# Gathered experts in units of 32 tokens: one row table for both matrices, masks from a unit matrix, quadrants added at a unit's end

## The chip, the cores and the metric

The program runs on one core of a Trainium2 chip. The metric is the device time of one whole execution in microseconds (us), the median of several runs. The engines are TensorE (PE in the profile, PEld its weight loads), VectorE (DVE), ScalarE (ACT), GpSimd (POOL) and SyncE (SP, here only a queue that issues DMAs). PSUM is TensorE's output memory; a DMA moves data between device memory and the on-chip SBUF.

## The reference

The program computes one layer of an encoder for 1,024 prompt tokens and 64 sample tokens, all in float32. The last part of the layer, a mixer over 16,384 tiny experts, takes most of the time and is what the change concerns. Each token chooses 128 experts (8 heads, 16 each); an expert is one row of `peer_u` and one row of `peer_v`, 1,024 wide.

```python
eid = jnp.take_along_axis(cid.reshape(PEER_BLOCK, PEER_HEADS, -1), ci, axis=-1)
gate = jax.nn.softmax(cv, axis=-1).reshape(PEER_BLOCK, -1)
...
u = jnp.take(peer_u, eid, axis=0)
vv = jnp.take(peer_v, eid, axis=0)
a = jax.nn.gelu(jnp.einsum('td,ted->te', xb, u).astype(jnp.float32), approximate=False) * gate
return jnp.einsum('te,ted->td', a.astype(xb.dtype), vv)
```

## The kernel before

The early stages (projection, mixers, routing, a matrix of gates in device memory) end at about 1,770 us of the trace. Then `experts` does the expert mixer in two ways side by side.

**Dense tokens.** For 512 prompt tokens all 16,384 experts are computed, in 64 steps of 256 experts. A float32 product is made of three matmuls of a high part and a low part of each factor. In a step TensorE does 48 matmuls of the U phase (`psum_u`), then 48 of the V phase for the experts of the step before, in 8 groups of 6, each into one bank of `psum_v`. There are 3 such banks: the fourth group of a V phase can only start when VectorE has added the first group's bank into `y`. Around that, in each step: ScalarE applies gelu to each half of the U phase (`act_f`) and writes its high part (`a_hi`), VectorE multiplies by the gates and writes the low part (`a_lo`); when the U phase is over, ScalarE makes the high part of the next U weights (`u_hi`), VectorE the low part (`u_lo`), and after `u_lo` VectorE comes to the eight additions to `y`.

**Gathered tokens.** For the other 512 prompt tokens and the 64 sample tokens only the chosen rows are fetched. GpSimd issues indirect DMAs, each of 128 rows of 4 KB (512 KB): 576 of `u` rows into 6 buffers, 576 of `v` rows into 10. A unit is 64 tokens. On a `u` fetch VectorE does one dot product of 128 rows with the tokens' vectors in `h2n` (one instruction over 128x1024). For `u`, the 128 partitions hold 64 tokens twice (two slots of each), so a unit takes 64 fetches; for `v`, a fetch holds the 128 slots of one token. Between the two the activations must be turned over: once in a unit, ScalarE applies gelu, VectorE multiplies by the gates, TensorE transposes (`turned_g`) and ScalarE copies (`weight`). Then, for every 4 tokens, ScalarE writes 4 masks of 32 columns (one column scaled by the token's weights, the others zero) and TensorE does a **quad**: 8 matmuls with those masks against 4 fetched `v` buffers, which sum up rows in `psum_g`. A tile of 128 tokens is added to `xg` by VectorE and stored (5 tiles in all). The first 80 fetches of `u` come before the first of `v`.

**The order.** Every engine runs its own queue in program order. A class `Timetable` weaves the gathered work into the dense steps: it gives each step 10 places on VectorE, 4 on ScalarE and 4 on TensorE, and puts an item in the first place after its due time (masks in the last place before). 18 fetches (9 of `u`, 9 of `v`) fall due in a step. VectorE's place 3 lies between the gate product of a step's second half and its `a_lo`, place 4 between that `a_lo` and `u_lo`, place 5 between `u_lo` and the first addition to `y`. ScalarE's place 2 lies between the second `a_hi` and `u_hi`. TensorE's place 1 lies between the U and the V phase.

Of the kernel before, what the change touches and what calls it, by code (L numbers as in the profile page):

```python
# [7 lines left out]
F32 = mybir.dt.float32  # L8
# [47 lines left out]
GT = 4  # L56
# [366 lines left out]
def route(nc, hg, hd, router, iota, sel_i, sel_j, sel_g, eid_u, eid_v, gate_n):  # L423

    with ExitStack() as ctx:
# [58 lines left out]
        sel_turned, sel_out = sem("sel_turned"), sem("sel_out")  # L484
        block = ctx.enter_context(nc.Block())
# [10 lines left out]
        def _(act):  # L496
# [39 lines left out]
            for s, dst in enumerate((sel_g, sel_i, sel_j)):  # L536
                act.wait_ge(sel_turned, s + 1)
                for c in range(3):
                    n = min(4, NT - 4 * c)
                    last = nc.scalar.activation(dst[:, 4 * c * P:(4 * c + n) * P],  # L540
                                                (qp if s % 2 == 0 else sp_.ap().rearrange("p c a b -> p c (a b)"))
                                                [:, c, 0:n * P], ACT.Copy)
                last.then_inc(sel_out, 1)

        @block.tensor
        def _(pe):
# [33 lines left out]
            for s, n in enumerate((2, 0, 1)):  # L580
                if s == 0:
                    pe.wait_ge(final.sem, final.at(PH - 1, "gate"))
                elif s == 1:
                    pe.wait_ge(look.sem, look.at(PH - 1, "key"))
                else:
                    pe.wait_ge(key_sum, PH)
                    pe.wait_ge(sel_out, 1)
                for t in range(NT):
                    bank = (qp[:, t // 4, (t % 4) * P:(t % 4 + 1) * P] if s % 2 == 0 else sp_[:, t // 4, t % 4, :])
                    last = nc.tensor.transpose(bank, chosen[:, n, t, :], ident[:, :])  # L590
# [3 lines left out]
        def _(dve):  # L594
# [144 lines left out]
            first, second_key, weight = (chosen[:, n, 0:GT, :].rearrange("p t s -> p (t s)") for n in range(3))  # L739
# [4 lines left out]
            def by_unit(out, tiles, sample):  # L744

                units = out[:, 0:DBASE].rearrange("p (t u s) -> p t u s", u=2, s=DEC)
                for token_half, slot_half in ((0, 0), (0, 1), (1, 0), (1, 1)):
                    here, there = (slice(DEC * h, DEC * h + DEC) for h in (token_half, slot_half))
                    nc.vector.tensor_copy(units[there, :, token_half, :], tiles[here, :, there])
                for slot_half in range(2):  # L750
                    there = slice(DEC * slot_half, DEC * slot_half + DEC)
                    last = nc.vector.tensor_copy(out[there, DBASE:GTOK], sample[0:DEC, there])
                return last
            by_unit(gate_n, chosen[:, 2, 0:GT, :], chosen[:, 2, PT, :])
            dve.wait_ge(named, 1)
            by_unit(eid_u, eid_f, rest[:, PT, :]).then_inc(named, 1)
            dve.wait_ge(named, 2)
            dve.wait_ge(sel_out, 3)
            eid_g = rest[:, 0:GT + 1, :].rearrange("p t n -> p (t n)")
            expert_of(eid_g[:, 0:DBASE], sel_i[:, 0:DBASE], sel_j[:, 0:DBASE])  # L760
            expert_of(eid_g[:, DBASE:GTOK], sel_i[:, SEQ:TOK], sel_j[:, SEQ:TOK]).then_inc(named, 1)
            dve.wait_ge(named, 3)
            nc.vector.tensor_copy(eid_v[:, :], eid_g[:, 0:GTOK]).then_inc(named, 1)
# [41 lines left out]


class FirstExperts:
# [9 lines left out]
    def gathered(self, nc, ctx):  # L817

        self.ident = ctx.enter_context(nc.sbuf_tensor("ex_ident", [P, P], F32))
        self.spike = ctx.enter_context(nc.sbuf_tensor("ex_spike", [P, 2 * VQ - 1], F32))  # L820
# [8 lines left out]
def gate_matrices(nc, sel_i, sel_j, sel_g, iota, gates, u, ahead, u_rows, eid_u, h2_units, ident_d, spike_d):  # L829

    with ExitStack() as ctx:
# [32 lines left out]
        def _(sp):  # L864
            sp.dma_start(ahead.u_raw[:, :, :, :], u[0]).then_inc(ahead.u_loaded, 16)
            for n in range(2):
                sp.dma_start(ahead.h2n[0:DEC, n, :], h2_units[n]).then_inc(ahead.h2_loaded[n], 16)
# [1457 lines left out]
```

## Time and profile before

| what | value |
|---|---|
| time, median of 3 runs (lowest to highest) | 3763.81 us (3763.61 to 3769.61) |
| time of the profiled execution | 3769.68 us |
| span of its trace | 3767.9 us |
| TensorE busy, all of the span | 3246.0 us (86%) |
| VectorE busy | 2486.4 us (66%) |
| ScalarE busy | 1090.4 us (29%) |
| GpSimd busy | 1725.7 us (46%) |
| mean transfer rate over the span | 243 GB/s |

The span goes from the first to the last instruction in the trace; the time of the execution contains it. Busy shares are means over stages that have different limits, so the stages are read apart: the experts take from about 1,770 us to the end.

### The profile page before, as it was taken

What the parts mean: (1) busy time and instruction counts of PE and PEld (TensorE: products, weight loads), DVE (VectorE), ACT (ScalarE), POOL (GpSimd) and SP (SyncE); (2) the same over time, 40 slices, a digit from 0 to 9 for tenths busy, and PEclk for the clock granted to TensorE, in tenths of its full rate; (3) what the DMA queues carried; (4) which work ended last, traced back from release to release, by engine and by line L of the source; (5) the groups of instructions that cost most, each with busy time, mean ns of one, the idle gap of its engine ahead of it and who ended that gap; (6) DMA issues with size and microseconds to landing.
All of it is one profiled execution on the core that took longest, in us unless ns stands there. A gap on an engine that the chain in (4) does not pass through costs nothing. (4 is left out here: it accounts for less than half of the span.)

```text
span 3767.9 us, 46521 instructions
## 1 busy us (share of the span) xinstructions
PE 3246.0 (86%) x16946; PEld 2480.5 (66%) x16946; DVE 2486.4 (66%) x5661; ACT 1090.4 (29%) x2113; POOL 1725.7 (46%) x1354
## 2 busy tenths in 40 slices
PE   5999778899984889487679999999988999999997
PEld 4888657777773777486456666666666666666654
DVE  3100167776742699996887777777777778777743
ACT  3111133443432211186112222222222222222321
POOL 1000000000001144385777777677777877777754
PEclk7999889999987888798889999999999999999999
DMA  5222211111112100078999999999999999999997
GB/s 140 91 86 86 112 51 46 57 40 37 49 39 82 55 28 23 0 217 250 343 363 400 406 406 406 404 409 395 411 396 410 409 405 407 407 411 408 396 345 281
DMA packets 300403, 914.37 MB, mean 243 GB/s; under 512 B 27430, under 2 KB 111326, under 8 KB 282540
## 3 DMA queue, kind: packets, MB, share of 16 engines
q0 software_dynamic: 168048, 612.53, 41.9%
q1 hardware_dynamic: 132156, 299.25, 22.0%
q8 instruction: 117, 1.92, 0.2%
q14 instruction: 82, 0.67, 0.1%
HBM read 848.57 MB, written 64.32 MB: 242 GB/s over the span
## 5 line engine op out<-in xcount | busy, mean ns | idle before, releaser
L1142 POOL DMA_INDIRECT ex_row_u<-in_u_rows,eid_u x570 | 746.9, 1310 | 303.1 <-issue 169.1
L1151 POOL DMA_INDIRECT ex_row_v<-in_v_rows,eid_v x576 | 694.9, 1206 | 245.5 <-issue 168.9
L1219 DVE CUSTOM_DVE_ANT_0 ex_row_u<-ex_row_u,ex_h2n 128x1024 f32<-128x1024 f32 x576 | 705.1, 1228 | 22.8 <-DMA ex_row_u<-in_u_rows,eid_u 21.9
L1330 PE MATMUL ex_psum_v<-ex_a_hi,ex_v_hi 128*128 128x512 f32 x1024 | 428.2, 418 | 170.3 <-DVE ex_y L1272 150.9
L395 POOL DMA_DIRECT2D rt_w_raw<-in_wq x2 | 1.1, 534 | 1111.1 <-POOLq L1543 1111.1
L1272 DVE TENSOR_TENSOR ex_y<-ex_y,ex_psum_v 128x512 f32<-128x512 f32 x504 | 332.5, 682 | 149.0 <-PE ex_psum_v L1330 125.6
L1314 PE MATMUL ex_psum_u<-h2d_hi,ex_u_hi 128*128 128x512 f32 x1024 | 410.4, 401 | 19.7 <-DVE ex_u_lo L1260 14.5
L1330 PE MATMUL ex_psum_v<-ex_a_lo,ex_v_hi 128*128 128x512 f32 x1024 | 414.4, 405 | 0.0
L1330 PE MATMUL ex_psum_v<-ex_a_hi,ex_v_lo 128*128 128x512 f32 x1024 | 413.9, 404 | 0.0
L1314 PE MATMUL ex_psum_u<-h2d_lo,ex_u_hi 128*128 128x512 f32 x1024 | 402.3, 393 | 0.0
L1314 PE MATMUL ex_psum_u<-h2d_hi,ex_u_lo 128*128 128x512 f32 x1024 | 399.9, 390 | 0.0
L1330 PEld LDWEIGHTS ex_psum_v<-ex_a_hi,ex_v_hi 128*128 128x128 f32 x1024 | 198.4, 194 | 298.7 <-DVE ex_y L1272 177.8
L1191 ACT ACTIVATE ex_v_hi<-ex_v_raw 128x2048 fp32r<-128x2048 f32 x64 | 122.7, 1917 | 736.2 <-PE ex_psum_v L1330 546.4
L1298 PE MATMUL ex_psum_g<-ex_row_v,ex_mask 128*32 128x512 f32 x2304 | 302.4, 646 | 23.3 <-DMA ex_row_v<-in_v_rows,eid_v 23.3
L1251 DVE TENSOR_TENSOR ex_act_f<-ex_act_f,ex_gate 128x512 f32<-128x512 f32 x128 | 88.6, 692 | 333.4 <-ACT ex_act_f L1199 185.7
L1314 PEld LDWEIGHTS ex_psum_u<-h2d_hi,ex_u_hi 128*128 128x128 f32 x1024 | 193.0, 189 | 123.7 <-issue 69.1
L1199 ACT ACTIVATE ex_act_f<-ex_psum_u 128x512 f32<-128x512 f32 x128 | 76.4, 597 | 558.9 <-PE ex_psum_u L1314 460.0
L1330 PEld LDWEIGHTS ex_psum_v<-ex_a_hi,ex_v_lo 128*128 128x128 f32 x1024 | 200.5, 196 | 45.2
L1330 PEld LDWEIGHTS ex_psum_v<-ex_a_lo,ex_v_hi 128*128 128x128 f32 x1024 | 199.7, 195 | 37.6
L1314 PEld LDWEIGHTS ex_psum_u<-h2d_hi,ex_u_lo 128*128 128x128 f32 x1024 | 193.3, 189 | 42.3
L1314 PEld LDWEIGHTS ex_psum_u<-h2d_lo,ex_u_hi 128*128 128x128 f32 x1024 | 193.3, 189 | 37.9
L332 DVE TENSOR_TENSOR pj_w_lo<-pj_w_raw,pj_w_hi 128x3600 fp32r<-128x3600 f32 (+1 forms) x7 | 27.3, 3899 | 273.1 <-ACT pj_w_hi L318 273.1
(324 smaller groups left out, 5767.6 us busy)
## 6 DMA issues: line engine op xcount, KB each, us to landing
ex_u_raw<-in_u SPq DMA_DIRECT2D x64, 1024.0 KB
ex_v_raw<-in_v SPq DMA_DIRECT2D x64, 1024.0 KB
gates<-gt_out SPq DMA_DIRECT2D x8, 4096.0 KB
ex_gate<-gates SPq DMA_DIRECT2D x64, 512.0 KB
mx_pj<-proj SPq DMA_DIRECT2D x9, 1796.0 KB, 7.3
proj<-pj_out SPq DMA_DIRECT2D x63, 225.0 KB, 2.1
pj_w_raw<-in_w_in SPq DMA_DIRECT2D x6, 1800.0 KB, 7.8
ex_row_u<-in_u_rows,eid_u POOLq DMA_INDIRECT x576
```

Source lines behind the costliest of these rows:

```text
L332: nc.vector.tensor_tensor(w_lo[:, 1 - par, :, 0:w], w_raw[:, :, 0:w], w_hi[:, 1 - par, :, 0:w].bitcast(F32), ALU.subtract).then_inc(w_low, 1)
L395: pool.dma_start(self.w_raw[:, p, :, :], self.wq[p]).then_inc(self.w_first, 16)
L1142: nc.gpsimd.indirect_dma_start(row_u[:, r % UR, :], None, u_rows, bass.IndirectOffsetOnAxis(eid_u[:, r:r + 1], 0)).then_inc(u_row[r % UR], 16)
L1151: nc.gpsimd.indirect_dma_start(row_v[:, r % VR, :], None, v_rows, bass.IndirectOffsetOnAxis(eid_v[:, V_TOK[r]:V_TOK[r] + 1], 0)).then_inc( ...
L1191: nc.scalar.activation(v_hi[:, :, :], v_raw[:, :, :], ACT.Copy).then_inc(v_high, 1)
L1199: nc.scalar.activation(act_f[:, i % 2, :], psum_u[:, i % 2, :], ACT.Gelu).then_inc(active, 1)
L1219: nc.vector.tensor_tensor_reduce(row_u[:, r % UR, :], row_u[:, r % UR, :], h2n[:, n % 2, :], 1.0, 0.0, ALU.mult, ALU.add, dots[:, n % 2, r ...
L1251: nc.vector.tensor_tensor(by_block, by_block, gate[:, :, j, :], ALU.mult).then_inc(gated, 1)
L1272: ins = nc.vector.tensor_tensor(y[:, d, :], y[:, d, :], psum_v[:, i % VB, :], ALU.add)
L1298: last = nc.tensor.matmul(psum_g[VQ * q:VQ * (q + 1), half, :], mask[:, k % MR, q, :], row_v[:, (4 * k + q) % VR, half * 512:(half + 1) * ...
L1314: last = nc.tensor.matmul(psum_u[:, i % 2, :], a[:, j, k, :], b[:, k, :], start=(m == 0), stop=(m == 3 * KD - 1))
L1330: last = nc.tensor.matmul(psum_v[:, i % VB, :], a[:, j, d * P:(d + 1) * P], b[:, (s - 1) % 2, j, :], start=(m == 0), stop=(m == 3 * JG - 1))
```

## The change

A unit is now 32 tokens, and a fetch, of `u` and of `v` alike, holds four slots of each of them: partition 32q+t is slot quarter q of token t. One table of row numbers, `eid`, serves both fetches, and the gates lie in the same layout, so nothing is turned over.

- The transposes, the `weight` copies and VectorE's gate products are gone. GpSimd multiplies four stacked 32x32 unit matrices (`eye`) by the gates, one 128x128 product for every 4 fetches of `v` (144 in all), which writes the masks' first form. ScalarE then applies gelu to the 4 columns of dots (128x4) and scales the 4 masks in place.
- The vectors of a unit must lie four times over the partitions: 3 ScalarE copies of 32x1024 per unit (16 units), where VectorE made one copy per unit of 64.
- At the end of a unit of 8 quads, the four quadrants of `psum_g` are partial sums of the same 32 tokens: VectorE copies the two banks to SBUF (128x1024), TensorE adds the quadrants with two matmuls against `eye` (a fold), VectorE adds the result (64x512) to `xg`. 18 of each, where 5 additions of 128x1024 stood.
- `v` fetches start at once, with 6 `u` fetches of lead in place of 80.
- In the routing, all tokens' choices were transposed and are now for the dense tokens only; 24 copies each on ScalarE and VectorE lay out gates and row numbers.

The table that places the dots keeps its rule and its 10 places, but its fetches are counted from another origin. Over all steps, the dots per place (places 0 to 9) were 64, 63, 63, 59, 63, 4, 65, 65, 65, 65 and are 63, 63, 65, 1, 65, 64, 64, 64, 64, 63. ScalarE's place 2 held the masks of 32 quads; it holds those of 15 quads and 13 copies of `h2n`. TensorE's place 1 held 34 quads and holds 32. Of all quads, 22 came after the `u_lo` of step 59, and now 12 do.

The order of VectorE's instructions in one step, from the gate product of the second half on, before (`ISA` with `ex_row_u` is a dot, the row behind it reads its sum):

```order
L1251 TENSOR_TENSOR ex_act_f<-ex_act_f,ex_gate 128x512
L1219 ISA ex_row_u,ex_dots<-ex_row_u,ex_h2n 128x1024
L1219 ISA ex_dots 128x1
L1255 TENSOR_TENSOR ex_a_lo<-ex_act_f,ex_a_hi 128x512
L1219 ISA ex_row_u,ex_dots<-ex_row_u,ex_h2n 128x1024
L1219 ISA ex_dots 128x1
L1260 TENSOR_TENSOR ex_u_lo<-ex_u_raw,ex_u_hi 128x2048
L1272 TENSOR_TENSOR ex_y<-ex_y,ex_psum_v 128x512 x2
```

The same stretch of VectorE's queue in the changed kernel:

```order
L1234 TENSOR_TENSOR ex_act_f<-ex_act_f,ex_gate 128x512
L1238 TENSOR_TENSOR ex_a_lo<-ex_act_f,ex_a_hi 128x512
L1204 ISA ex_row_u,ex_dots<-ex_row_u,ex_h2n 128x1024
L1204 ISA ex_dots 128x1
L1243 TENSOR_TENSOR ex_u_lo<-ex_u_raw,ex_u_hi 128x2048
L1204 ISA ex_row_u,ex_dots<-ex_row_u,ex_h2n 128x1024
L1204 ISA ex_dots 128x1
L1255 TENSOR_TENSOR ex_y<-ex_y,ex_psum_v 128x512 x2
```

One dot has moved from ahead of `a_lo` to between `u_lo` and the first addition to `y`.

ScalarE's queue around `u_hi` in one of the steps with a mask ahead of it, before:

```order
L1199 ACTIVATE ex_act_f<-ex_psum_u 128x512
L1159 ACTIVATE ex_a_hi<-ex_act_f 128x512
L1181 ACTIVATE ex_mask<-ex_spike,ex_weight 128x32 x4
L1205 ACTIVATE ex_u_hi<-ex_u_raw 128x2048
L1181 ACTIVATE ex_mask<-ex_spike,ex_weight 128x32 x4
```

And in a step of the changed kernel that has both a mask and a copy of `h2n` there:

```order
L1184 ACTIVATE ex_act_f<-ex_psum_u 128x512
L1153 ACTIVATE ex_a_hi<-ex_act_f 128x512
L1158 ACTIVATE ex_dots<-ex_dots 128x4
L1162 ACTIVATE ex_mask<-ex_mask,ex_dots 128x32 x4
L1167 ACTIVATE ex_h2n<-ex_h2n 32x1024
L1190 ACTIVATE ex_u_hi<-ex_u_raw 128x2048
L1167 ACTIVATE ex_h2n<-ex_h2n 32x1024
```

The gelu of the dots and the copies are new in this place. On GpSimd the queue was nothing but fetches in turn; now a product stands behind every fourth `v` fetch:

```order
L1138 DMA ex_row_v<-in_v_rows,eid 128x1024
L1145 TENSOR_TENSOR ex_mask<-ex_eye,gate_n 128x128
L1131 DMA ex_row_u<-in_u_rows,eid 128x1024
L1138 DMA ex_row_v<-in_v_rows,eid 128x1024
L1131 DMA ex_row_u<-in_u_rows,eid 128x1024
```

What moved there is only the product, which the two kinds of fetch now wait behind.

The diff of `Timetable` and of the gathered work, cut to its core:

```diff
-    AHEAD = DEC + 16
...
-        self.fetches = [("u", r) for r in range(self.AHEAD)]
-        for r in range(GTOK):
-            if r + self.AHEAD < GTOK:
-                self.fetches.append(("u", r + self.AHEAD))
-            self.fetches.append(("v", r))
-        place = {f: n for n, f in enumerate(self.fetches)}
+        self.fetches = [("u", f) for f in range(UR)]
+        for f in range(GTOK):
+            self.fetches.append(("v", f))
+            if f + UR < GTOK:
+                self.fetches.append(("u", f + UR))
+        place = {f: n - UR for n, f in enumerate(self.fetches)}
...
+        for k in range(QUADS):
+            for f in range(4 * k, 4 * k + 4):
+                ready = self.put("dve", self.dots, (place["u", f] + self.DUE) / self.PER, f)
+            made = self.put("act", self.masks, ready + 0.03, k)
+            due = max(made + 0.05, now, (place["v", 4 * k + 3] + self.DUE) / self.PER)
...
+            now = self.put("pe", self.quads, due, k)
+            unit = k // UQ
+            if k % UQ == UQ - 1:
+                free = self.put("dve", self.unloads, now, unit)
+                self.put("dve", self.adds, self.put("pe", self.folds, free, unit), unit)
+                self.read[int(ready)] = unit
+                later = ready + 1.6
+                for s in range(1, 4 if unit + 2 < UNITS else 1):
+                    later = self.put("act", self.copies, later + 0.01, (unit + 2, s))
```

```diff
+                        if f % 4 == 0:
+                            if k >= MR:
+                                pool.wait_ge(quad_done, k - MR + 1)
+                            nc.gpsimd.tensor_tensor(mask[:, k % MR, :, :], eye[:, :].unsqueeze(1).to_broadcast([P, 4, VQ]),
+                                                    gate_n[:, f:f + 4].unsqueeze(2).to_broadcast([P, 4, VQ]),
+                                                    ALU.mult).then_inc(gate_masked, 1)
...
                     for k in table.masks.get((s, place), ()):
+                        act.wait_ge(dotted, 4 * k + 4)
+                        nc.scalar.activation(dots[:, k % DR, :], dots[:, k % DR, :], ACT.Gelu).then_inc(g_active, 1)
+                        act.wait_ge(gate_masked, k + 1)
+                        act.wait_ge(g_active, k + 1)
                         for q in range(4):
-                            tok = q * UQ + k % UQ
-                            last = nc.scalar.activation(mask[:, k % MR, q, :], spike[:, VQ - 1 - m:2 * VQ - 1 - m],
-                                                        ACT.Copy, scale=weight[:, n % 2, tok:tok + 1])
+                            last = nc.scalar.activation(mask[:, k % MR, q, :], mask[:, k % MR, q, :], ACT.Copy,
+                                                        scale=dots[:, k % DR, q:q + 1])
                         last.then_inc(masked, 1)
...
+                    for n in table.unloads.get((s, place), ()):
+                        dve.wait_ge(quad_done, UQ * (n + 1))
+                        if n >= 1:
+                            dve.wait_ge(folded, n)
+                        nc.vector.tensor_copy(quadrants[:, :, :], psum_g[:, :, :]).then_inc(unloaded, 1)
...
+                    for n in table.folds.get((s, place), ()):
+                        pe.wait_ge(unloaded, n + 1)
+                        if n >= 1:
+                            pe.wait_ge(g_added, n)
+                        for half in range(2):
+                            last = nc.tensor.matmul(psum_f[VQ * half:VQ * half + VQ, :], eye[:, :], quadrants[:, half, :],
+                                                    start=True, stop=True)
+                        last.then_inc(folded, 1)
```

## Rows read from the trace of the kernel before

**Rows 1.** Windows: busy us of PE, PEld, DVE, ACT, POOL; clock, DMA share, GB/s.

```profile
1800.00:1850.00 50.00, 24.05 (x96) 19.07 (x96) 44.44 (x67) 8.62 (x8) 38.71 (x26) 0.79 0.95 348
...
3000.00:3200.00 200.00, 185.64 (x890) 127.87 (x891) 153.85 (x223) 56.21 (x108) 149.94 (x122) 0.97 1.02 406
```

**Rows 2.** Waits, 2200 to 3400 us (40 steps): us in total, times, longest.

```profile
PE ex_psum_v L1330 <- DVE ex_y L1272: 92.0, 40, 3.6
...
POOL ex_row_u L1142 <- DVE ex_dots L1219: 62.0, 50, 3.5
...
POOL ex_row_v L1151 <- PE ex_psum_g L1298: 22.8, 13, 3.6
...
DVE ex_row_u L1219 <- DMA ex_row_u<-in_u_rows,eid_u: 2.2, 1, 2.2
PE ex_psum_g L1298 <- DMA ex_row_v<-in_v_rows,eid_v: 1.9, 1, 1.9
```

**Rows 3.** Groups on GpSimd, 2200 to 3400 us: busy, mean ns | idle before.

```profile
L1142 POOL DMA_INDIRECT ex_row_u<-in_u_rows,eid_u x360 | 463.1, 1286 | 172.5 <-issue 110.5 <-DVE ex_dots L1219 62.0
L1151 POOL DMA_INDIRECT ex_row_v<-in_v_rows,eid_v x360 | 435.2, 1209 | 131.7 <-issue 108.9 <-PE ex_psum_g L1298 22.8
```

**Rows 4.** Timeline of a step with a mask ahead of `u_hi`: start, us, engine.

```profile
3005.26 0.39 PE L1314 MATMUL ex_psum_u<-h2d_hi,ex_u_lo 128*128 128x512 f32 x1
...
3006.93 1.22 DVE L1219 CUSTOM_DVE_ANT_0 ex_row_u<-ex_row_u,ex_h2n 128x1024 f32<-128x1024 f32 x1
...
3007.58 0.94 ACT L1181 ACTIVATE ex_mask<-ex_spike,ex_weight 128x32 f32<-128x32 f32 x4
...
3008.43 1.90 ACT L1205 ACTIVATE ex_u_hi<-ex_u_raw 128x2048 fp32r<-128x2048 f32 x1
...
3008.68 1.22 DVE L1219 CUSTOM_DVE_ANT_0 ex_row_u<-ex_row_u,ex_h2n 128x1024 f32<-128x1024 f32 x1
...
3010.36 2.29 DVE L1260 TENSOR_TENSOR ex_u_lo<-ex_u_raw,ex_u_hi 128x2048 fp32r<-128x2048 f32 x1 [0.46 <-issue]
...
3012.57 1.28 DVE L1272 TENSOR_TENSOR ex_y<-ex_y,ex_psum_v 128x512 f32<-128x512 f32 x2
...
3013.30 0.57 PE L1330 MATMUL ex_psum_v<-ex_a_hi,ex_v_hi 128*128 128x512 f32 x1 [3.57 <-DVE ex_y L1272]
...
3013.68 0.63 PE L1330 MATMUL ex_psum_v<-ex_a_lo,ex_v_hi 128*128 128x512 f32 x1
```

**Rows 5.** Timelines of TensorE, VectorE and ScalarE, the next step.

```profile
3036.64 0.39 PE L1314 MATMUL ex_psum_u<-h2d_hi,ex_u_lo 128*128 128x512 f32 x1
3036.96 1.92 PE L1298 MATMUL ex_psum_g<-ex_row_v,ex_mask 128*32 128x512 f32 x16
...
3044.14 0.50 PE L1330 MATMUL ex_psum_v<-ex_a_hi,ex_v_hi 128*128 128x512 f32 x1 [0.91 <-DVE ex_y L1272]
...
3038.96 1.90 ACT L1205 ACTIVATE ex_u_hi<-ex_u_raw 128x2048 fp32r<-128x2048 f32 x1
...
3041.20 2.29 DVE L1260 TENSOR_TENSOR ex_u_lo<-ex_u_raw,ex_u_hi 128x2048 fp32r<-128x2048 f32 x1
```

**Rows 6.** Timeline of VectorE: `u_lo` of steps 2, 6 and 59.

```profile
1846.67 2.29 DVE L1260 TENSOR_TENSOR ex_u_lo<-ex_u_raw,ex_u_hi 128x2048 fp32r<-128x2048 f32 x1
...
1984.77 2.28 DVE L1260 TENSOR_TENSOR ex_u_lo<-ex_u_raw,ex_u_hi 128x2048 fp32r<-128x2048 f32 x1
...
3578.52 2.29 DVE L1260 TENSOR_TENSOR ex_u_lo<-ex_u_raw,ex_u_hi 128x2048 fp32r<-128x2048 f32 x1 [0.46 <-ACT ex_u_hi L1205]
```

**Rows 7.** GpSimd's product in the gate stage (groups); a fetch beside `u_lo` (timeline).

```profile
L915 POOL TENSOR_TENSOR gt_gate_j<-gt_hot_j,sel_g 128x512 f32<-128x512 f32 x128 | 129.0, 1037 | 44.6 <-DVE gt_hot_j L897 43.9 <-issue 0.2
...
3642.89 2.29 DVE L1260 TENSOR_TENSOR ex_u_lo<-ex_u_raw,ex_u_hi 128x2048 fp32r<-128x2048 f32 x1 [1.96 <-issue]
...
3643.30 2.69 POOL L1151 DMA_INDIRECT ex_row_v<-in_v_rows,eid_v  x1 [0.30 <-PE ex_psum_g L1298]
```

**Rows 8.** Timeline of TensorE near the end: the last quads.

```profile
3737.22 3.59 PE L1298 MATMUL ex_psum_g<-ex_row_v,ex_mask 128*32 128x512 f32 x16 [7.01 <-DMA ex_row_v<-in_v_rows,eid_v]
```

More of the change, by code:

```diff
@@ L537, in _ @@
                 act.wait_ge(sel_turned, s + 1)
[L538 to L543, printed above, removed]
+                nc.scalar.activation(dst[:, :], qp[:, s, 0:DTOK], ACT.Copy).then_inc(sel_out, 1)
+                if s == 0:
+                    for there, here in fetch_parts(gate_n, chosen[:, 2, 0:GT, :], chosen[:, 2, PT, :]):
+                        nc.scalar.activation(there, here, ACT.Copy)
         @block.tensor
@@ L586, in _ @@
                     pe.wait_ge(key_sum, PH)
[L587 to L590, printed above, removed]
+                for t in range(GT, PT):
+                    last = nc.tensor.transpose(qp[:, s, (t - GT) * P:(t - GT + 1) * P], chosen[:, n, t, :], ident[:, :])
                 last.then_inc(sel_turned, 1)
@@ L742, in _ @@
             expert_of(rest[:, PT, :], chosen[:, 0, PT, :], chosen[:, 1, PT, :]).then_inc(named, 1)
[L744 to L754, printed above, removed]
-            dve.wait_ge(named, 1)
[L756 to L763, printed above, removed]
+            dve.wait_ge(named, 1)
+            for there, here in fetch_parts(eid, eid_f, rest[:, PT, :]):
+                nc.vector.tensor_copy(there, here)
         @block.gpsimd
@@ L804 @@
 MR = 4
+DR = 4
 class FirstExperts:
@@ L1037, in experts @@
     table = Timetable()
-    V_TOK = [DEC * n + q * UQ + m for n in range(UNITS) for m in range(UQ) for q in range(4)]
     with ExitStack() as ctx:
@@ L1183, in gathered @@
                         last.then_inc(masked, 1)
+                    for n, quarter in table.copies.get((s, place), ()):
+                        act.wait_ge(h2_loaded[n % 2], 64 + 16 * (n // 2))
+                        nc.scalar.activation(h2n[VQ * quarter:VQ * quarter + VQ, n % 2, :], h2n[0:VQ, n % 2, :],
+                                             ACT.Copy).then_inc(h2_copied, 1)
                 act.wait_ge(id_loaded, 32)
@@ L1232, in gathered @@
+                def gathered(s, place):
+                    for f in table.dots.get((s, place), ()):
+                        dot(f)
+                    for n in table.unloads.get((s, place), ()):
[3 more added lines that the diff above has]
+                        nc.vector.tensor_copy(quadrants[:, :, :], psum_g[:, :, :]).then_inc(unloaded, 1)
                     for n in table.adds.get((s, place), ()):
-                        dve.wait_ge(quad_done, QBASE[n] + TQ[n])
```

241 lines of the change are left out of this document (99 added, 142 removed).

## The prediction

> **What bounds the kernel now.** I read the busy shares in a few windows first. In the long middle TensorE is busy 185.6 us of 200, VectorE 153.9, GpSimd 149.9, ScalarE 56.2, at a granted clock of 0.97, close to the higher level of 2.4 GHz; the DMA share reads 1.02 and the rate is flat at 406 GB/s [rows 1]. TensorE and the transfers are both candidates, so the list of waits decides. In 1,200 us TensorE waits in one place: 92.0 us, 40 times, that is once in each of 40 steps, with the fourth group of a V phase for the first addition to `y` [rows 2]. Rows are hardly waited for: 2.2 us by a dot and 1.9 us by a quad [rows 2]. GpSimd does wait, 62.0 us for dots and 22.8 for quads to free its buffers [rows 2], so it is ahead of its consumers. The bound is TensorE plus that one wait of 92.0/40 = 2.30 us a step. The step is 1200/40 = 30.0 us there; from the `u_lo` of step 6 to that of step 59 it is (3578.52 − 1984.77)/53 = 30.07 [rows 6].
>
> The timeline shows what the wait consists of. I count from t0, the start of the last U matmul. With a mask ahead of `u_hi`: t0 = 3005.26; the mask at 3007.58 holds `u_hi` back to 3008.43, VectorE does two dots meanwhile, `u_lo` starts at 3010.36 (t0 + 5.10), the first addition 2.21 later, and TensorE resumes 0.73 after that, having waited 3.57 [rows 4]. Without a mask but with a quad before the V phase: `u_hi` ends at 3038.96 + 1.90 = t0 + 4.22, VectorE comes to `u_lo` at t0 + 4.56, and TensorE, which had the quad to do, waits 0.91 [rows 5]. The two kinds share the steps about evenly (mean 2.24 against the 2.30 measured). Any time by which the first addition comes later is therefore TensorE's, for it waits in every step.
>
> Two stretches differ. Around 1,800 us VectorE is busy 44.4 of 50 us and TensorE 24.1 [rows 1]: only `u` rows are fetched there, 18 dots fall in a step, and the step takes (1984.77 − 1846.67)/4 = 34.5 us [rows 6]. At the end, quads remain when little dense work does, and one of them waits 7.01 us for its rows [rows 8].
>
> **The change, part by part.**
>
> *The moved dot.* It is the term that decides. The dot at place 3 leaves and one at place 5 appears, in nearly all steps. A dot holds VectorE for 1.14 us (3006.93 to the `a_lo` that follows; its 1.22 overlaps the next). Ahead of `u_lo` its leaving helps little: without a mask `u_lo` then waits for `u_hi`, so it starts at about t0 + 4.26 instead of 4.56; with a mask it waited for `u_hi` already. Behind `u_lo` it counts whole: the first addition stands 2.21 + 1.14 = 3.35 behind the start of `u_lo`. The items ahead of `u_hi` on ScalarE change too. A mask gets a gelu of 128x4 before it; I take 0.2 us, near a quarter of the 0.94 for four mask copies [rows 4], which makes `u_lo` start at 5.2 or 5.3. A copy of 32x1024 is half as wide as `u_hi` (1.90), so about 1.0, and gives about 5.1. With 28 such steps of 64 the mean start is (36×4.26 + 28×5.2)/64 = 4.67, before it was (5.10 + 4.56)/2 = 4.83. The first addition moves from 7.04 to 4.67 + 3.35 = 8.02, by +0.98. Nine unloads and additions ahead of `u_lo` in some steps (about 1.2 and 0.7 each, /64, partly covered) make it **+1.06 a step**, so the wait should read about 3.4. The bounds are 0 (the additions turn out to be hidden) and +1.5 (place 2's items cost double).
>
> *The clock after a longer wait.* After the 3.57 wait the matmuls take 0.63 where they take 0.39 otherwise [rows 4, 5], for some six to eight of them, on the way from the lower of the clock's two levels (1.2 GHz) to the higher; after 0.91 only the first is longer (0.50). More steps get the long wait. I take **+0.2 a step**, between 0 and 0.9.
>
> *The folds.* 18 times two matmuls of 512 columns in float32 on a 64-row stack. A quad has 8 of these, four side by side, in 1.92 [rows 5]; two not side by side cost between 0.97 (as two quarter-sets) and 1.94. I take 1.3: 18×1.3/64 = **+0.37**. The transposes and their waits give back **−0.1**. VectorE's 18 unloads and additions, and the layout copies, lie in its idle 46 us of 200 [rows 1]; without that cover they would be 34 us in all.
>
> *GpSimd's products.* 2.25 a step. The nearest row is the product of the gate stage, 1.04 us for 128x512 [rows 7]: a quarter of it by elements is 0.26, with the usual gap of 0.30 after an instruction 0.56. From above: a fetch that stood beside `u_lo` took 2.69 where others take 0.94 [rows 7, 4], so with its gap 3.0. I take 1.0, nearer to the row of the same operation. GpSimd's own time a step is now (1202.5 − 62.0 − 22.8)/40 = 27.9 us, where 1202.5 is busy plus idle of both fetch groups [rows 3, 2]. It becomes 27.9 + 2.25 = 30.1 against a step of 31.6, so the products are hidden by GpSimd's own slack, of which the longer step makes more. They stop being hidden at (31.6 − 27.9)/2.25 = 1.64 each.
>
> The stretch of 2.69 beside a VectorE instruction with two SBUF inputs is what the Trainium skill (SBUF — State Buffer, Who interferes with whom) leads one to expect for a GpSimd instruction that reads SBUF: it and such a VectorE instruction share a read port, and the second to start blocks until the first is done. By that rule each product beside `u_lo`, `v_lo` or a dot waits for it, up to the 2.29 of `u_lo` [rows 7], or, if it starts first, holds VectorE up. The page infers that fetches are not held by such an instruction; the 2.69 here says that they are.
>
> *Start and end.* Quads begin with the first steps, so dots are spread 9 to a step and the first steps take 31.6 instead of 34.5: 4.5 such steps give 13, less a first wait for rows: **−12**. At the end 10 quads fewer follow the `u_lo` of step 59: 10×1.92 = 19, and the 7.0 wait goes [rows 8], against longer waits for `y` and the last unload, fold, addition and store, some 8: **−18**. Routing and its layout copies: 0, since removed and added copies are of like number, within ±5.
>
> Sum: per step 1.06 + 0.2 + 0.37 − 0.1 = 1.53, over 53 steps +81 (a step of 31.6); 81 − 12 − 18 = +51; I round to +48 for some cover of the folds under waits that exist anyway. On the profiled execution's 3769.7 that is 3818; it lies 5.9 above the median, so on the median **3812**.
>
> **Rivals.** 0.2%, 7.5 us, is about what a measurement of this kernel can tell from no change.
>
> *GpSimd becomes the bound (slower, more).* At 2.2 us a product the step is 27.9 + 5.0 = 32.9 instead of 31.6, +1.3×59 = +77 on top: 3889; at 3.0 it is 34.6 and near 3990. For it: a stretch of 2.69 is seen, and a late `v` row delays quads, which free buffers later. Against: the gate-stage row. Point of decision 1.64 us. Chance 0.16. The Trainium skill (GPSIMD Engine Reference, 4.1 Engine selection) speaks for this rival: it puts elementwise products of two inputs on VectorE, since GpSimd is about twice as slow at them; no run here shows the two engines on the same product.
>
> *The transfers are the bound (faster).* If the flat 406 GB/s is all there is, the step of 30.0 is the transfers' and TensorE's wait only fills it up; a later addition then costs nothing as long as work and wait fit in 30.0, the folds replace wait, and only the ends remain: −12 − 18 + a few = −27, so **3737**. For it: a share of 1.02 that does not move. Against: dots and quads wait 4.1 us in 1,200 for rows [rows 2], and GpSimd waits for buffers, not the other way round. It decides if TensorE's added 1.5 us a step come out of waits elsewhere. Chance 0.17.
>
> *In between.* Half of the shift is hidden, 3764 ± 7: 0.08 for a time within 0.2%, and a little more on either side, in the cases above.
>
> **The numbers.** The forecast with its own bounds (per step +0.9 to +1.9, ends −20 to −36: 3785 to 3850) has 0.59, GpSimd 0.16, the transfers 0.17, between 0.08. The range reaches from inside the transfers' case, 3745, to GpSimd's at 2.2 us, 3885, and leaves out the rest of both, some 0.2. Faster 0.17, same 0.08, slower 0.75.
>
> **What would show it.** In the changed trace: the wait of the fourth V group for `y` about 3.4 a step and in every step; 3.35 from `u_lo` to the first addition; a step of 31.6 between the `u_lo` of steps 6 and 59; GpSimd's product about 0.7 long and GpSimd still waiting for dots; rows still hardly waited for. Wrong it is if the product takes over 1.6, if quads or dots wait for rows by more than 0.5 us a step, or if the step stays near 30.0 with the dot in its new place.

## The result and the profile after

The changed kernel takes 3823.65 us (median of 4 runs, 3815.13 to 3828.85), the kernel before 3764.01: a ratio of 1.0147 over all runs of the two, with a 95% interval of 1.0125 to 1.017 (the quotient of the two medians is 1.0158). It is slower, by 59.6 us of the medians where 48 were forecast (3812), and inside the range. The profiled execution took 3823.41 us, its span is 3821.6, 53.7 more than before.

VectorE's queue shows where the steps of 256 experts lie. The `u_lo` of steps 6 and 59, in the timeline of VectorE after the change:

```profile
1951.31 2.28 DVE L1243 TENSOR_TENSOR ex_u_lo<-ex_u_raw,ex_u_hi 128x2048 fp32r<-128x2048 f32 x1
...
3650.07 2.29 DVE L1243 TENSOR_TENSOR ex_u_lo<-ex_u_raw,ex_u_hi 128x2048 fp32r<-128x2048 f32 x1
```

Against [rows 6] this cuts the 53.7 us into four parts. The step-0 `u_lo` starts at 1764.56 (before 1778.91): −14.4. From there to step 6 it takes 186.8 (before 205.9): −19.1. The 53 steps from 6 to 59 take 1698.8 (before 1593.8): +105.0, that is 32.05 a step in place of 30.07. What follows takes 171.5 (before 189.4): −17.9.

Two windows, busy us of the engines, clock, DMA share and GB/s, as in [rows 1]:

```profile
1800.00:1850.00 50.00, 47.08 (x225) 31.81 (x226) 40.15 (x59) 13.66 (x29) 41.26 (x34) 0.97 1.00 395
...
3000.00:3200.00 200.00, 178.00 (x838) 120.68 (x837) 144.92 (x203) 61.87 (x115) 156.65 (x127) 0.95 0.99 384
```

The early stretch, which VectorE bound before, is now like the others (TensorE busy 47.1 of 50, before 24.1). In the middle every engine but GpSimd and ScalarE is busy for less of the time, the granted clock is 0.95 for 0.97, and the rate, flat at 406 GB/s before, has fallen to 384. The list of waits from 2,200 to 3,400 us, which answers to [rows 2]:

```profile
PE ex_psum_v L1315 <- DVE ex_y L1255: 130.9, 38, 6.2
...
POOL ex_row_v L1138 <- PE ex_psum_g L1275: 52.4, 17, 6.0
...
POOL ex_row_u L1131 <- DVE ex_dots L1204: 36.9, 29, 3.5
```

TensorE waits in the same place as before, now 3.49 us a step (130.9 over 37.5 steps) in place of 2.30. No wait of a dot or a quad for a row is in the list at all. GpSimd still waits 89 us for buffers. Its groups in the same stretch, answering to [rows 3], have the product as a third line:

```profile
L1131 POOL DMA_INDIRECT ex_row_u<-in_u_rows,eid x339 | 450.2, 1328 | 119.6 <-issue 82.1 <-DVE ex_dots L1204 36.9
L1138 POOL DMA_INDIRECT ex_row_v<-in_v_rows,eid x338 | 422.2, 1249 | 150.2 <-issue 97.8 <-PE ex_psum_g L1275 52.4
...
L1145 POOL TENSOR_TENSOR ex_mask<-ex_eye,gate_n 128x128 f32<-128x128 f32 x84 | 57.5, 685 | 1.5
```

And one step in the timeline, with a mask ahead of `u_hi`, to be laid beside [rows 4]:

```profile
2392.49 0.40 PE L1299 MATMUL ex_psum_u<-h2d_hi,ex_u_lo 128*128 128x512 f32 x1
...
2394.82 0.19 ACT L1158 ACTIVATE ex_dots<-ex_dots 128x4 f32<-128x4 f32 x1
...
2395.10 0.96 ACT L1162 ACTIVATE ex_mask<-ex_mask,ex_dots 128x32 f32<-128x32 f32 x4
...
2395.96 1.90 ACT L1190 ACTIVATE ex_u_hi<-ex_u_raw 128x2048 fp32r<-128x2048 f32 x1
...
2397.90 2.29 DVE L1243 TENSOR_TENSOR ex_u_lo<-ex_u_raw,ex_u_hi 128x2048 fp32r<-128x2048 f32 x1 [1.12 <-ACT ex_u_hi L1190]
2400.11 1.22 DVE L1204 CUSTOM_DVE_ANT_0 ex_row_u<-ex_row_u,ex_h2n 128x1024 f32<-128x1024 f32 x1
...
2401.25 1.28 DVE L1255 TENSOR_TENSOR ex_y<-ex_y,ex_psum_v 128x512 f32<-128x512 f32 x2
...
2401.99 0.80 PE L1315 MATMUL ex_psum_v<-ex_a_hi,ex_v_hi 128*128 128x512 f32 x1 [4.96 <-DVE ex_y L1255]
2402.58 0.63 PE L1315 MATMUL ex_psum_v<-ex_a_lo,ex_v_hi 128*128 128x512 f32 x1
...
2404.85 3.10 PE L1275 MATMUL ex_psum_g<-ex_row_v,ex_mask 128*32 128x512 f32 x16
```

`u_lo` starts 5.41 after the last U matmul, the first addition 3.35 after `u_lo` (before 2.21), with the dot in between; TensorE waits 4.96. Behind the wait matmuls take 0.63, and the quad that comes then takes 3.10 where one takes 1.92 otherwise [rows 5].

### The profile page after: what moved, and what is told of

Read it like the earlier page. It is cut to its first block and busy times, and to the rows that moved or that the text cites. A ratio compares the mean times of both kernels' runs of the same rounds, so it can differ in the third digit from the quotient of the medians.

```text
span 3821.6 us, 47329 instructions
## 1 busy us (share of the span) xinstructions
PE 3285.4 (86%) x16994; PEld 2482.3 (65%) x16994; DVE 2524.8 (66%) x5674; ACT 1177.8 (31%) x2296; POOL 1856.6 (49%) x1498
## 5 line engine op out<-in xcount | busy, mean ns | idle before, releaser
L1131 POOL DMA_INDIRECT ex_row_u<-in_u_rows,eid x570 | 757.3, 1329 | 206.3 <-issue 138.7
L1138 POOL DMA_INDIRECT ex_row_v<-in_v_rows,eid x576 | 714.8, 1241 | 274.3 <-issue 165.9
L1204 DVE CUSTOM_DVE_ANT_0 ex_row_u<-ex_row_u,ex_h2n 128x1024 f32<-128x1024 f32 x576 | 713.3, 1239 | 7.0 <-DMA ex_row_u<-in_u_rows,eid 7.0
L1275 PE MATMUL ex_psum_g<-ex_row_v,ex_mask 128*32 128x512 f32 x2304 | 317.0, 674 | 31.1 <-DMA ex_row_v<-in_v_rows,eid 29.7
## 6 DMA issues: line engine op xcount, KB each, us to landing
gates<-gt_out SPq DMA_DIRECT2D x8, 4096.0 KB, 16.8
```

Of the source, the lines that this page charges most:

```text
L1131: nc.gpsimd.indirect_dma_start(row_u[:, f % UR, :], None, u_rows, bass.IndirectOffsetOnAxis(eid[:, f:f + 1], 0)).then_inc(u_row[f % UR], 16)
L1138: nc.gpsimd.indirect_dma_start(row_v[:, f % VR, :], None, v_rows, bass.IndirectOffsetOnAxis(eid[:, f:f + 1], 0)).then_inc(v_row[f % VR], 16)
L1204: nc.vector.tensor_tensor_reduce(row_u[:, f % UR, :], row_u[:, f % UR, :], h2n[:, n % 2, :], 1.0, 0.0, ALU.mult, ALU.add, dots[:, k % DR, ...
L1275: last = nc.tensor.matmul(psum_g[VQ * q:VQ * (q + 1), half, :], mask[:, k % MR, q, :], row_v[:, (4 * k + q) % VR, half * 512:(half + 1) * ...
```

## The experiments

Each was timed beside the kernel before on the same chip. Where a theory speaks of the changed kernel, 1.0147 is to be compared.

**1. The dot moved back.** Added at the end of `Timetable`'s constructor:

```diff
+        moved = {}
+        for (s, place), rows in sorted(self.dots.items()):
+            moved.setdefault((s, {4: 3, 5: 4}.get(place, place)), []).extend(rows)
+        self.dots = moved
```

> The changed kernel with one table rule added: VectorE's dots of place 5 stand at place 4 and those of place 4 at place 3, where the kernel before had them; all else is as in the changed kernel. Theory (the dot behind u_lo is what TensorE pays for): the first addition to y comes 2.2 after the start of u_lo in place of 3.35, u_lo itself some 0.15 later, so the wait for y falls from 3.45 to about 2.4 a step, the step from 32.05 to about 30.7, and the time by 53 x 1.3 = 70 us to about 3750 (3735 to 3770), under the kernel before. Rival (the lost time is the new work: products, folds, copies, and transfers that come at 384 GB/s): the step stays above 31.5 and the time above 3795.

Measured: 3745.99, a ratio of 0.9951 (0.9932 to 0.997). The wait for `y` is 2.57 a step, the step 30.76. The kernel is faster than before by 19 us (0.5%), with all of the rest of the change in it.

**2. The dot moved late, alone.** The same lines in the kernel before, with `{3: 4, 4: 5}`.

> The kernel before with the same dot moved the other way: its dots of place 3 stand at place 4, those of place 4 at place 5, behind u_lo. Nothing else of the change is made. Theory: the wait for y rises from 2.3 to about 3.3 a step, the step from 30.07 to about 31.4, and the time by 60 x 1.3 = 78 us to about 3840 (3815 to 3865). Rival (the place of the dot is covered, the new work costs): within 10 us of 3764.

Measured: 3842.89, a ratio of 1.0203 (1.0182 to 1.0224): +77 from the order of one instruction. The wait for `y` in the list of waits (2,200 to 3,400 us) of this kernel, and of the first experiment under it:

```profile
PE ex_psum_v L1335 <- DVE ex_y L1277: 124.5, 38, 4.8
```

```profile
PE ex_psum_v L1320 <- DVE ex_y L1260: 101.9, 39, 5.1
```

The two runs agree: the dot's place costs 77 us in the kernel before and 78 in the changed one (3823.65 − 3745.99; 74 by the two ratios), and the rest of the change gives 18 to 21 in both orders.

**3. No products on GpSimd.** ScalarE writes masks from the unit matrix.

```diff
-                        act.wait_ge(gate_masked, k + 1)
+                        if k >= MR:
+                            act.wait_ge(quad_done, k - MR + 1)
...
-                            last = nc.scalar.activation(mask[:, k % MR, q, :], mask[:, k % MR, q, :], ACT.Copy,
+                            last = nc.scalar.activation(mask[:, k % MR, q, :], eye[:, :], ACT.Copy,
```

> The changed kernel without GpSimd's products: ScalarE scales the unit matrix by the activations and writes the masks from it, in the same four instructions, so the gates are left out of the result. Theory (GpSimd has slack, 0.7 us a product is hidden): within 10 us of 3824. Rival (GpSimd or the read port that it shares is the bound): 2.25 x (0.7 + 0.1) = 1.8 us a step come back, 3824 - 100 = about 3720.

Measured: 3822.68, a ratio of 1.0148 (1.0131 to 1.0165). The step stays at 32.00. GpSimd only waits longer for dots, in the list of waits from 2,200 to 3,400 us (36.9 us in the changed kernel): what the products took was slack.

```profile
POOL ex_row_u L1131 <- DVE ex_dots L1197: 104.7, 74, 3.7
```

**4. Three additions ahead of `u_lo`.** In VectorE's queue:

```diff
+                    for d in range(EARLY):
+                        add_y(s, d)
                     if s + 1 < GROUPS:
                         dve.wait_ge(u_high, s + 2)
...
-                    gathered(s, 5)
-                    for d in range(KD):
...
-                        if d % 2 == 1:
-                            gathered(s, 6 + d // 2)
+                    for d in range(EARLY, KD):
+                        add_y(s, d)
+                        gathered(s, d - EARLY + 5)
```

> The changed kernel with the first three additions to y ahead of u_lo on VectorE; the items of places 5 to 9 follow one by one behind the later additions. Theory: TensorE's wait for y ahead of the fourth group goes (3.45 a step) and with it most of the slow matmuls after it (0.6); a wait for a later group may appear, and the transfers (12.06 MB a step) cannot be faster than about 29.7 us a step at the 406 GB/s seen before, so the step falls to 29.5 to 30.3 and the time to about 3700 (3670 to 3740). Rival (TensorE's wait only fills time that transfers or GpSimd set): rows are waited for instead and the step stays near 32, the time above 3800.

Measured: 3714.56, a ratio of 0.9856 (0.9836 to 0.9876). The step is 30.47, a little over what was expected. Its list of waits, 2,200 to 3,400 us:

```profile
DVE ex_row_u L1204 <- DMA ex_row_u<-in_u_rows,eid: 95.3, 71, 4.6
...
PE ex_psum_g L1280 <- DMA ex_row_v<-in_v_rows,eid: 63.9, 27, 6.1
...
PE ex_psum_v L1320 <- DVE ex_y L1232: 23.5, 20, 3.8
POOL ex_row_u L1131 <- DVE ex_dots L1204: 15.3, 9, 4.8
...
POOL ex_row_v L1138 <- PE ex_psum_g L1280: 1.5, 5, 0.3
```

Most of the wait for `y` is gone (0.54 a step is left), and more than half of what it gave back went into waits for rows (1.73 a step of TensorE's). GpSimd waits for almost nothing: 16.8 us of 1,200. So the wait for `y` was the bound, and behind it stands another one, at about 30 us a step. Experiments 7, 8, 10, 11 and 12 ask which.

**5. No folds.** TensorE's two matmuls a unit are left out, and VectorE adds from the copy in SBUF:

```diff
-                        dve.wait_ge(folded, n + 1)
+                        dve.wait_ge(unloaded, n + 1)
...
-                        nc.vector.tensor_tensor(xg[:, n % 2, :], xg[:, n % 2, :], psum_f[0:2 * VQ, :],
+                        nc.vector.tensor_tensor(xg[:, n % 2, :], xg[:, n % 2, :], quadrants[0:2 * VQ, 0, :],
```

> The changed kernel without the fold's matmuls: VectorE adds the first two quadrants straight to the tokens, so the sums of the last two are left out. Theory (a fold costs TensorE 0.31 us a step, 1.1 each, and a little of the clock): 3824 - 20 = about 3804 (3795 to 3812). Rival (the folds lie in waits that are there anyway): within 5 us of 3824.

Measured: 3813.64, a ratio of 1.0122 (1.0105 to 1.0139), between the theory and the rival: 9.4 us less than the changed kernel by the ratios, with intervals that still overlap. In the traces the step goes from 32.05 to 31.85: 0.31 of folds goes and 0.09 comes back as a longer wait for `y` (3.42 to 3.51).

**6. The token loads in halves, as before.** The loads ahead of the routing again go through the function that cuts each tile of 128 rows into two loads of 64, in pieces of 16.

```diff
-                normed_transposed(nc, "n2", x2_tile, I["ln2"], part(g_hi, hd[0]), part(g_lo, hd[1]), ident_d, eps_d,
+                normed_transposed(nc, "n2", in_units, I["ln2"], part(g_hi, hd[0]), part(g_lo, hd[1]), ident_d, eps_d,
```

> The changed kernel with the token loads ahead of the routing as the kernel before had them: each tile of 128 tokens in two loads of 64 rows, taken in pieces of 16 (the tokens then lie in another order, so each result goes to the wrong token; the work is the same). Theory (these loads are where the 14 us before the first step came from): 3824 + 13 = about 3837 (3830 to 3845). Rival (the gain came from the shorter transposes or from layout copies): within 5 us of 3824.

Measured: 3841.53, a ratio of 1.0194 (1.0172 to 1.0215), 18 us more. The step is unchanged at 32.05. ScalarE's wait for these tiles, in the list of waits from 1,180 to 1,262 us, of this kernel and of the changed one:

```profile
ACT n_junk L156 <- DMA n_x<-x: 32.1, 8, 16.0
```

```profile
ACT n_junk L156 <- DMA n_x<-x: 16.4, 8, 8.7
```

The 15.7 us between them are most of the 19.1 by which the step-0 `u_lo` starts later here (1783.64) than in the changed kernel. So the gain ahead of the first step comes in the main from a line of the diff that the prediction did not price.

**7. Additions ahead, no products.** The fourth and the third experiment together.

> The kernel with three additions ahead of u_lo, without GpSimd's products (ScalarE writes the masks from the unit matrix, the gates are left out of the result). Theory: with TensorE's wait gone GpSimd is the bound there, since it waits only 17 us of 1,200; without the products (0.77 us each and their gaps, some 2 us a step) the step falls from 30.47 to about 29.0 and the time from 3715 to about 3640 (3620 to 3675). Rival (the transfers are the bound): within 15 us of 3715.

Measured: 3686.72, a ratio of 0.979 (0.9773 to 0.9808). A step is 29.75: the products do cost there, 25 us by the two ratios, but a third of what was expected, and rows are still waited for (1.49 a step). The time lies outside the theory's range and the rival's.

**8. Additions ahead, products on VectorE.** Nothing left out; the product stands behind every fourth dot.

```diff
+                        if f % 4 == 0:
+                            k = f // 4
+                            if k >= MR:
+                                dve.wait_ge(quad_done, k - MR + 1)
+                            nc.vector.tensor_tensor(mask[:, k % MR, :, :], eye[:, :].unsqueeze(1).to_broadcast([P, 4, VQ]),
+                                                    gate_n[:, f:f + 4].unsqueeze(2).to_broadcast([P, 4, VQ]),
+                                                    ALU.mult).then_inc(gate_masked, 1)
```

> The kernel with three additions ahead of u_lo, with the products on VectorE, one behind every fourth dot, and 5 mask buffers for 4; nothing is left out. A product of 128x128 costs VectorE about a quarter of the 0.69 of one of 128x512, with its start 0.25, 0.6 us a step of VectorE's slack. Theory (GpSimd is the bound of that kernel): close to the same kernel without products, about 3650 (3625 to 3690). Rivals: the transfers are the bound, 3700 to 3730; VectorE's products delay the additions, above 3730.

Measured: 3699.34, a ratio of 0.9816 (0.98 to 0.9832). It computes the reference and is the fastest version that does, 1.8% under the kernel before. The 50 us of the theory did not come; the time is the one that the rival of the transfers gave (3700 to 3730), which experiment 11 tests. GpSimd's groups of this kernel, 2,200 to 3,400 us, to be compared with those of experiments 11 and 12:

```profile
L1138 POOL DMA_INDIRECT ex_row_v<-in_v_rows,eid x361 | 490.6, 1359 | 110.0 <-issue 108.8 <-PE ex_psum_g L1279 1.2
L1131 POOL DMA_INDIRECT ex_row_u<-in_u_rows,eid x361 | 476.5, 1320 | 124.6 <-issue 107.9 <-DVE ex_dots L1196 16.7
```

**9. The dot back, and ScalarE's place 2 empty.** To the edit of the first experiment comes one in the list of places:

```diff
-        self.times = {e: [(s + f, s, n) for s in range(self.steps) for n, f in enumerate(fs)]
+        self.times = {e: [(s + f, s, n) for s in range(self.steps) for n, f in enumerate(fs)
+                          if (e, n) != ("act", 2)]
```

> The changed kernel with the dots moved back as in the first experiment, and with ScalarE's place 2 left empty: masks and copies of h2n that fell there go to place 3, behind u_hi. Theory (what stands ahead of u_hi delays the first addition as the dot did, where VectorE does not): u_hi ends at 4.2 in every step, the wait for y falls from 2.57 to about 2.0, and the time from 3746 to about 3720 (3705 to 3735); GpSimd, with 29 to 30 us of its own work a step, may take some of it back. Rival (place 2 is covered by VectorE's two dots): within 8 us of 3746.

Measured: 3717.98, a ratio of 0.9866 (0.9847 to 0.9884). What stands ahead of `u_hi` costs too, as the theory had it: the step goes from 30.76 to 30.28. The wait for `y` falls by half of what was expected, from 2.57 to 2.28; the quads give most of the rest (4.63 to 4.42 a step). GpSimd waits 4.3 us of 1,200 for buffers here and dots wait 23.5 for rows, so the second bound is near.

**10. The kernel before with three additions ahead of `u_lo`.** The edit of experiment 4, except in the 9 steps or fewer where a unit's gate product falls into place 6 or 7, which there stays ahead of the fifth addition:

```diff
+                    soon = (s, 6) in table.gates or (s, 7) in table.gates
+                    for d in range(EARLY, KD):
+                        add_y(s, d)
+                        for place in ({3: (5, 6, 7), 5: (8,), 7: (9,)}.get(d, ()) if soon else (d - EARLY + 5,)):
+                            gathered(s, place)
```

> The kernel before with three additions ahead of u_lo on VectorE, and none of the change. Theory: its wait of 2.3 a step goes too, and rows are waited for in its place; since no products stand on GpSimd the step comes to 29.4 to 29.8 in place of 30.07, the time to about 3735 (3715 to 3755): less is won than in the changed kernel, and the changed kernel with the same edit, 3715, stays ahead by its shorter start and end. Rival (in the kernel before nothing but that wait stands in the way): 30.07 - 2.3 - 0.3 = 27.5 a step, about 3620.

Measured: 3749.31, a ratio of 0.995 (0.9934 to 0.9966), a step of 29.89. With the same edit the changed kernel gains 109 us and this one 16. With the wait for `y` out of the way the change is 35 us the better one (0.9856 against 0.995), by its start, its first steps and its end; its step is 0.58 longer (30.47 against 29.89). What bounds the kernel before at 29.89 is open: TensorE waits 68.4 us of 1,200 for rows there at 408 GB/s, while GpSimd waits 97.3 for buffers.

**11. Half the bytes, as many fetches.** In the kernel of experiment 8:

```diff
-                            row_u[:, f % UR, :], None, u_rows,
+                            row_u[:, f % UR, cols], None, u_rows.rearrange("r (h d) -> (r h) d", h=2),
```

with `cols` the first 512 columns, and the same for `v`.

> The kernel with additions ahead of u_lo and products on VectorE, with fetches of half as many bytes: each gathers 128 half rows of 2 KB; the dots and quads are as long as before, on data that is half stale. As many fetches are issued, for half the bytes. Theory A (the transfers are what bounds it at 404 GB/s): row waits go, the step falls from 29.98 to about 28.4, the time from 3699 to about 3605 (3585 to 3640), and a fetch takes GpSimd less than the 1.33 us of there. Theory B (GpSimd's issue is the bound, held by VectorE's instructions with two inputs): a fetch still takes 1.3, the step stays above 29.6 and the time above 3675.

Measured: 3700.28, a ratio of 0.9822 (0.9781 to 0.9863): as experiment 8. Window (engines, clock, share, GB/s) and GpSimd's groups of this kernel:

```profile
3000.00:3200.00 200.00, 184.31 (x904) 127.99 (x903) 158.74 (x240) 67.09 (x128) 163.11 (x122) 1.00 0.77 254
```

```profile
L1132 POOL DMA_INDIRECT ex_row_u<-in_u_rows,eid x362 | 501.0, 1384 | 110.3 <-issue 108.8 <-DVE ex_dots L1198 1.5
L1140 POOL DMA_INDIRECT ex_row_v<-in_v_rows,eid x362 | 480.7, 1328 | 110.4 <-issue 109.2 <-PE ex_psum_g L1281 1.2
```

The rate is 254 GB/s, the share 0.77, and the step still 29.83: the transfers do not bound this kernel. GpSimd does, for it waits 2.7 us of 1,200 and needs (1.36 + 0.30) x 18 = 29.9 us for a step's fetches. In experiment 8, with all bytes, the same sum gives (1.34 + 0.30) x 18 = 29.5 of a step of 29.98; that the transfers set a bound close by there is not excluded.

**12. Dots with one input.** In the kernel of experiment 8 again, with full rows:

```diff
-                    nc.vector.tensor_tensor_reduce(row_u[:, f % UR, :], row_u[:, f % UR, :], h2n[:, n % 2, :], 1.0, 0.0,
-                                                   ALU.mult, ALU.add, dots[:, k % DR, f % 4:f % 4 + 1]).then_inc(dotted, 1)
+                    nc.vector.tensor_reduce(dots[:, k % DR, f % 4:f % 4 + 1], row_u[:, f % UR, :], mybir.AxisListType.X,
+                                            ALU.add).then_inc(dotted, 1)
```

> The kernel with additions ahead of u_lo and products on VectorE, with its dots replaced by plain sums over the fetched rows: one input from SBUF instead of two, of the same 128x1024, some 1.2 us; the tokens' vectors are left out of the result. Theory (a fetch on GpSimd is held while VectorE runs an instruction with two SBUF inputs, and GpSimd's issue is what bounds that kernel): fetches beside a sum take the 0.95 that they take beside nothing, only those beside u_lo and v_lo stay long, so the mean of 1.34 falls to about 1.15, row waits of TensorE mostly go (1.6 a step), the step falls from 29.98 to 28.3 to 28.8 and the time from 3699 to about 3620 (3595 to 3645). Rival (a fetch is long for another reason): a mean of 1.3 and a time within 15 us of 3699.

Measured: 3658.6, a ratio of 0.9713 (0.9697 to 0.973). GpSimd's groups:

```profile
L1138 POOL DMA_INDIRECT ex_row_v<-in_v_rows,eid x369 | 411.0, 1114 | 112.6 <-issue 111.0 <-PE ex_psum_g L1279 1.6
L1131 POOL DMA_INDIRECT ex_row_u<-in_u_rows,eid x369 | 399.0, 1081 | 278.4 <-DVE ex_dots L1196 205.3 <-issue 73.1
```

A fetch takes 1.10 (1.34 in experiment 8), with VectorE's instruction as long as the dot was (1.21 and 1.22). GpSimd waits for buffers again, 205.3 us, so its issue is no longer the bound. The step is 29.40 and not the 28.5 of the theory: rows are still waited for, 1.41 a step, now at 416 GB/s and a share of 1.02. Whether the transfers are the bound there stays open; no run with few bytes and such dots was made.

## Why the prediction was right, and where it was off

**The mechanism.** The forecast's main theory holds step by step. The first addition to `y` stands 3.35 behind `u_lo`, the wait reads 3.49 against the 3.4 that were announced, and experiments 1 and 2 move the time by 74 to 78 us in either direction with that one dot. Both opposite rivals are out as the changed kernel stands: the transfers' (the rate fell to 384 GB/s and no row was waited for) and GpSimd's (experiment 3, where taking the products out changes nothing). GpSimd's comes back once the wait for `y` is out of the way (experiments 4, 7 and 11).

**The sum a step.** TensorE's time in the 53 steps, taken apart by what lies between the start of one matmul and the next, in us a step (0.2265 is the distance of two dense matmuls that run on without a wait at the higher clock level):

```
                                before   after   change   forecast
wait for y                       2.28     3.42    +1.14    +1.06
dense matmuls beyond 0.2265      1.36     1.77    +0.41  \  +0.2
quads                            4.54     4.77    +0.23  /
folds                            0.00     0.31    +0.31    +0.37
transposes, waits for them and
for rows                         0.10     0.00    -0.10    -0.1
dense matmuls at 0.2265 each    21.77    21.77     0.00     0.00
all                             30.07    32.05    +1.98    +1.53
```

The wait, the folds and the transposes were sized within 0.1. The term that was mis-sized is the clock after a longer wait: +0.2 was taken (0 to 0.9 allowed), and it measured 0.64. Two parts were too small. The dense matmuls alone took 0.41: those more than 0.3 apart are 9.4 a step where they were 8.1. And the prediction left out that a quad which follows the wait is slowed too (3.10 for 1.92 in the step shown): 29 of the 119 quads in these steps took over 2.2 us, before 20. The term goes with the wait: the excess of the dense matmuls and the quads together is 5.90 a step before and 6.54 after, and in the changed kernel with shorter waits it is 6.15 (experiment 1, wait 2.57) and 5.91 (experiment 9, wait 2.28, as before). Without the folds it stays (6.57, experiment 5). The matmuls' and quads' rows say that the clock was at its lower level for longer; the granted clock of the window fell from 0.97 to 0.95. Over 53 steps the difference of 0.45 makes 24 us.

**Start and end.** The end came as forecast (−17.9 for −18). The first steps gave 19.1 for 12: six of them took 31.1 each in place of 34.3, where the sum had put 4.5 at 31.6 and taken something off for a first wait. The start gave 14.4 where 0 within 5 was written: the step "routing and its layout copies" looked at transposes and copies, and passed over the token loads (experiment 6). The 14.4 is that of one pair of traces: in the ten traces with the changed kernel's stages ahead of the experts the step-0 `u_lo` starts between 1762.6 and 1773.5, in the three with the stages of before between 1774.1 and 1778.9, and the means differ by 9. In the pair, start and end together gave 51 us in place of 30, which took back 21 of the 24 us above. The median came out 11.6 above the forecast: 2.7 are left of the sum, 3 are its rounding from 51 to 48, and 5.9 lie between the median of the kernel before and its profiled execution. The agreement is partly luck, that of two errors.

**Small errors in the working.** The 28 steps with something ahead of `u_hi` add 15 and 13; four steps hold a mask and a copy, so there are 24, which takes 0.06 off the wait. The bounds 3785 to 3850 do not follow from the terms given with them: 0.9 and 1.9 a step over 53 steps, with −36 and −20 at the ends, give 3776 and 3845. The measured time lies inside both. The 0.94 of an undisturbed fetch is not in [rows 4], where 0.94 is the masks'; the table below has it.

**GpSimd's product.** It was taken at 1.0 with its gap and takes 0.69 with next to none ahead of it (0.41 at its shortest, 2.2 at its longest). VectorE needs 0.27 to 0.35 for the same product (experiment 8). The point at which it decides, 1.64, holds for a step of 31.6 only: with the wait for `y` out of the way (experiment 4), GpSimd waits for almost nothing at a step of 30.5 with products of 0.77, and taking them out gives 25 us (experiment 7).

**What a fetch waits for.** Fetches from 2,200 to 3,400 us of the kernel before (534 of 719) and of experiment 12 (560 of 737), grouped by what VectorE did beside them (mean us of one, and their number); those beside other instructions of VectorE are left out:

```
VectorE beside the fetch               before        dots with one input
nothing                                0.94 (144)    0.95 (104)
addition to y (one input in PSUM)      0.94 (98)     0.95 (75)
dot or sum alone                       1.50 (29)     0.94 (77)
dot or sum, and an addition to y       1.09 (139)    0.94 (186)
u_lo or v_lo                           2.03 (124)    1.69 (118)
```

What VectorE runs when the fetch starts decides. In the kernel before all 188 fetches that start while VectorE is idle take 0.94 or 0.95, whatever begins beside them. All 199 that start inside an instruction with two inputs in SBUF, more than 0.15 us ahead of its end, end 0.81 to 0.84 after it. Those that start as far inside an addition to `y` (41), or in experiment 12 inside a sum (177), take under 0.99. So a fetch is held when it starts inside an instruction with two inputs in SBUF, and the hold goes when the dot has only one. The sum also writes no row back, as the dot does; but the addition to `y` writes to SBUF and holds no fetch. No `u_lo` of these takes longer than 2.30, so a fetch that started first is not seen to slow VectorE down. The Trainium skill (SBUF — State Buffer, Who interferes with whom) says that a VectorE instruction with two SBUF inputs contends with a GpSimd instruction that reads SBUF and that the later one blocks; for the fetch that comes later, the rows here agree. It also infers that such an instruction does not stall the making of descriptors; 2.03 against 0.94 says otherwise for these gathers, and the measurement decides.

## What to carry to other kernels

Where one engine waits in every step for the same instruction of another, what is put ahead of that instruction can cost its full length, and the order can be worth more than the amount of work: here one dot of 1.14 us cost 77 us in 64 steps (1.2 a step, with the slower matmuls behind the longer wait), with no work added. When a change is woven in by a table of due times, compare the order that comes out around that instruction before judging the change itself; here the rest of the change was a gain of 19 us that its own table hid. And price every line of a diff in the stages that run before: loads cut in two cost 18 us (experiment 6), in a stage that the prediction had put at 0.

## What the runs showed of the hardware

- A gather of 128 rows takes GpSimd 0.94 us and a gap of 0.30, and up to 3.05 in the kernel before when it starts inside a VectorE instruction with two SBUF inputs. With half the bytes to move (experiment 11) the issue is as long as with all (1.36 against 1.34 in experiment 8). So GpSimd was the bound there at 250 GB/s.
- After 4.96 us of waiting the next matmuls took 0.63 to 0.80 in place of 0.39, and a quad 3.10 in place of 1.92.
- Four tiles of 128 rows, loaded in two pieces of 64 rows each in place of one, kept ScalarE waiting 32.1 us in place of 16.4. Whether the number of loads or their pieces of 16 rows does it was not tried.
